# Three edits to a two-block fp32 kernel on one core: semaphores cleared inside the next stage, the meta products of attention moved, the last expert units loaded into free places

## The chip, the cores and the metric

The kernel runs on 1 core of one Trainium2 chip. The metric is the device time of one execution in microseconds.

## The reference

Two transformer blocks in a row, fp32, batch 1, 512 tokens, width 1024. The first has stick-breaking attention (8 heads of 64) beside a gated linear attention (4 heads of 128), 16 meta tokens ahead of the sequence, and a mixture of 32 experts with two experts for each token. The second has a convolution branch, a state-space branch and a dense feed-forward part. Cut to what the change touches:

```python
def stick_breaking_attention(q, k, v):
    ...
        z = einsum('bhtd,bhsd->bhts', q[:, :, t0:t1], k[:, :, :t1]) * scale
        valid = (s_pos < t_pos) & (s_pos >= LEAD_PAD)
        log_keep = where(valid, log_sigmoid(-z), 0.0)
        log_tail = cumsum(log_keep, axis=3, reverse=True) - log_keep
        w = where(valid, exp(log_sigmoid(z) + log_tail), 0.0)
        outs.append(einsum('bhts,bhsd->bhtd', w, v[:, :, :t1]))

def hierarchical_moe(x2, ...):
    ...
    def run_block(args):
        tok, g, e = args
        xb = x2[tok]
        hb = silu(xb @ w_gate[e]) * (xb @ w_up[e])
        return (hb @ w_down[e]) * g[:, None]
```

## The kernel before

The program is a row of ten stages. Each is one `nc.Block()` in which SyncE (SP), ScalarE (ACT), VectorE (DVE), GpSimd (POOL) and TensorE (PE) have a program of their own and wait for one another by semaphores. They are: projections of the first block (block at L148), stick-breaking attention (L467), gated linear attention (L738), output projection and routing (L1000), the 32 experts (L1336), overflow blocks of the experts (L1563), the join of the two blocks (`join`, L1853), the groups of the state-space branch (L1990), the mix (L2550) and the feed-forward part (`ffn`, L2806). A block ends with a drain on each engine and a barrier in which GpSimd collects and releases the others. The profile puts these under the line where the stage's sources begin: L101 for the first stage, L1299 for the experts, L1554 for the overflow.

Behind each stage stands `g["clear"](...)` (L2904 to L2914): another block, in which GpSimd alone clears every semaphore of the stage, one instruction each (L2911), while the others go straight into that block's barrier (L2907). Then the semaphores go back to the pool, and the next stage takes them. The semaphores on which the gathers and scatters count (`g["gathers"]`) are cleared but not given back.

Attention (L418 to L712) works through 24 pieces, three per head. For a piece, TensorE forms the scores (`scores`, L479 a mask product, L484 products over 64 rows), ScalarE turns them into log terms (`front`, L553 to L557), VectorE adds (`sums`, L649 and L655), TensorE forms the sums over later keys by triangular matrices (`tails`, L492 to L507), ScalarE takes the exponential (`weights`, L572), and TensorE multiplies by the values (`values`, L519). Three pieces are kept in flight (AHEAD = 3), with six banks. The scores of the 16 meta keys of all heads are formed at once (L527, four fp32 products of 512 columns), and their values are spread (L530); both stand on TensorE between the first three `scores` and the loop, and their parts on ScalarE (`front_meta`, L561 to L565) and VectorE (`sums_meta`, `values_meta`, L659 and L664) stand at the same place. TensorE waits for five constants of GpSimd (`con`) ahead of the loop. ScalarE takes the logs of the forget gates (`log_forget`, L575) in the pieces 0 to 3; VectorE reads them from piece 6 on (`decays`).

The expert stage (L1294 to L1547) takes an expert's weights in six units of 1 MB: 0 and 1 of the gate, 2 and 3 of the up, 4 and 5 of the down matrix. Each unit number has its own place for the raw fp32 (`raw_e`), for the high part and for the low part. SP loads a unit when VectorE has made the low part of that place's last unit (L948). ScalarE copies it to the high part (`hi`, L1354), which waits until TensorE has used the place's last unit; VectorE subtracts (`lo`, L1422). TensorE runs, for expert e: `project` of the gate (L1498, L1499), `combine` of expert e-1 (L1512), the turning of the gathered rows (L1489), `project` of the up matrix, `down` of expert e-2 (L48 to L50). `down` waits for `y_out` of the expert before (L1394, ScalarE), and GpSimd gathers rows (L1460) and scatters the result (L1464). The loops run on after the last expert until nothing is left, so on ScalarE the end reads:

```python
for e in range(E + 3):
    hi(e + 1, 0); gate_out(e); hi(e - 2, 5); silu(e - 1); hi(e + 1, 1); y_out(e - 3)
    gathered(e + 1); hi(e + 1, 2); h_hi(e - 1); hi(e + 1, 3); up_out(e); hi(e - 1, 4)
```

The overflow stage reads on each engine, from `over_e`, how many overflow blocks there are, and passes over its body if there are none.

Of the kernel before, what the change touches and what calls it, by code (L numbers as in the profile page):

```python
# [5 lines left out]
ALU = mybir.AluOpType  # L6
# [10 lines left out]
NT = T // P  # L17
# [53 lines left out]
def stage_a(nc, dram, g, sem, banks):  # L71
# [5 lines left out]
    with ExitStack() as keep:  # L77
# [361 lines left out]
        with ExitStack() as tmp:  # L439
# [30 lines left out]
            def _(pe):  # L470
# [59 lines left out]
                mm(O, pick[:, :, :].rearrange("k h s -> k (h s)"), v_nat[0:META, NT, :], start=True, stop=True).then_inc(s["vr"], 1)  # L530
                pe.wait_ge(s["con"], 5)
                for n in range(NP):
                    if n + AHEAD < NP:
                        scores(n + AHEAD)
                    tails(n)
                    if n % 3 == 0 and n >= 3:
                        values(n // 3 - 1)
# [8 lines left out]
            def _(act):  # L546
# [34 lines left out]
                front_meta()  # L581
                for n in range(NP):
# [3 lines left out]
                    if n < HG_HEADS:  # L586
                        log_forget(n)
# [11 lines left out]
            def _(pool):  # L599
                gp = nc.gpsimd  # L600
# [32 lines left out]
            def _(dve):  # L633
# [84 lines left out]
        with ExitStack() as tmp:  # L718
# [138 lines left out]
            def _(pool):  # L857
                nc.gpsimd.memset(acc, 0.0).then_inc(s["cleared"], 1)
# [63 lines left out]
def stage_b(nc, dram, g, sem, banks):  # L922
# [23 lines left out]
    def load(sp, j, of):  # L946
        place = raw_e[j][:, :] if j < 4 else raw_e[j][:, :].rearrange("p (k c) -> p k c", k=2)
        sp.dma_start(place, unit_source(of, j)).then_inc(s_raw_e[j], 16)  # L948
# [7 lines left out]
    with ExitStack() as tmp:  # L956
# [66 lines left out]
        def _(pool):  # L1023
            nc.gpsimd.iota(iota[:, :], [[1, P]], 0, 0, allow_small_or_imprecise_dtypes=True).then_inc(s["io"], 1)
# [274 lines left out]
    with ExitStack() as tmp:  # L1299
# [24 lines left out]
        def made_hi(e, j):  # L1324
            return (s["ghi"], 4 * e + j + 1) if j < 4 else (s["dhi"], 2 * e + j - 3)

        def made_lo(e, j):
            return (s["glo"], 4 * e + j + 1) if j < 4 else (s["dlo"], 2 * e + j - 3)
# [7 lines left out]
        block = tmp.enter_context(nc.Block())  # L1336

        @block.sync
        def _(sp):
            for e in range(E + 2):  # L1340
                for at, j in ((e + 1, 0), (e - 2, 5), (e + 1, 1), (e + 1, 2), (e + 1, 3), (e - 1, 4)):
                    if 1 <= at < E:
                        sp.wait_ge(*made_lo(at - 1, j))
                        load(sp, j, at)

        @block.scalar
        def _(act):
            def hi(e, j):

                if 0 <= e < E:  # L1350
# [1608 lines left out]
```

## Time and profile before

| what | value |
|---|---|
| times of three runs, us | 2415.74, 2419.7, 4282.94 |
| median, us | 2419.7 |
| the profiled execution's own time, us | 2418.91 |
| its span, us | 2417.2 |
| mean granted clock of TensorE | 0.92 |
| busy: TensorE / its weight loads / VectorE / ScalarE / GpSimd | 87% / 69% / 58% / 45% / 8% |
| DMA, mean over the span | 144 GB/s |

The profile records one execution. Its span is counted from the first to the last instruction; the execution's own time is 1.7 us longer. Times in rows are us from the start of the span unless they are marked ns. Drains, semaphore instructions and DMA issues are not counted as busy. PE is TensorE's matmul, PEld its weight load; a letter q behind an engine's name is its instruction queue. A granted clock of 1.00 is 2.4 GHz, 0.50 is 1.2 GHz. A row for a stretch of time has its length, then for PE, PEld, DVE, ACT and POOL the busy time and in brackets the count of instructions, then the granted clock, the share in which the DMA engines were busy, and GB/s. A row in order of time begins with start and duration, and may end with the idle time before it and what ended that. A row for the instructions of one line has count, shortest/median/longest in ns, and the starts of the first and the last.

### The profile page before, as it was taken

Reading aid. Unit: us, or ns where it says so; the run is one execution under the profiler, and the core shown is the slowest. Engines: PE = TensorE matmul, PEld = TensorE weight load, DVE = VectorE, ACT = ScalarE, POOL = GpSimd, SP = SyncE. Lnnn points to the kernel's source line nnn. Section 1 sums busy time; section 2 is a strip of 40 time slices with the busy share of each in tenths; the row PEclk is TensorE's granted clock in tenths of the full one; section 3 lists DMA queues with packets and bytes.
Section 4 is the critical chain, followed back from the end, with each engine's and each line's share of the span. In section 5 each row is a group of like instructions: output and inputs, shape, how many; then the busy total and the mean of one; then the engine's idle time right before and its main releaser. Section 6 shows DMA issues by size and latency. Waiting matters only on the chain. (4 is left out here: it accounts for less than half of the span.)

```text
span 2417.2 us, 25574 instructions
## 1 busy us (share of the span) xinstructions
PE 2097.0 (87%) x10228; PEld 1665.3 (69%) x10228; DVE 1391.7 (58%) x1512; ACT 1084.2 (45%) x1229; POOL 189.0 (8%) x132
## 2 busy tenths in 40 slices
PE   5999966675899999993779999997698987999997
PEld 4886546563666666662668888886567866888786
DVE  4111468346899989883339898887733244333223
ACT  4232632224788888882333555544243224222212
POOL 0001021000222212220000000000000000000000
PEclk9998987766999999996689999998899998999999
DMA  4220000414999999984233333323132222333231
GB/s 153 70 70 1 1 0 1 160 61 183 380 399 406 405 401 402 401 337 167 53 89 87 91 102 88 87 71 87 35 105 87 87 70 74 92 105 87 87 105 52
DMA packets 202064, 346.89 MB, mean 144 GB/s; under 512 B 13872, under 2 KB 149544, under 8 KB 184536
## 3 DMA queue, kind: packets, MB, share of 16 engines
q1 hardware_dynamic: 191280, 332.49, 39.3%
q0 software_dynamic: 5120, 8.40, 1.1%
q10 hardware_dynamic: 5543, 4.34, 0.6%
q8 instruction: 82, 1.34, 0.2%
q14 instruction: 39, 0.31, 0.0%
HBM read 340.93 MB, written 12.65 MB: 146 GB/s over the span
## 5 line engine op out<-in xcount | busy, mean ns | idle before, releaser
L1422 DVE TENSOR_TENSOR wlo_e<-raw_e,whi_e 128x2048 fp32r<-128x2048 f32 x192 | 436.3, 2289 | 62.5 <-ACT whi_e L1354 62.2
L1354 ACT CAST whi_e<-raw_e 128x2048 fp32r<-128x2048 f32 x192 | 366.8, 1913 | 77.3 <-PE pall L1499 37.6
L1717 DVE TENSOR_TENSOR w_lo<-w_raw,w_hi 128x2048 fp32r<-128x2048 f32 x89 | 203.8, 2290 | 322.0 <-ACT w_hi L1709 322.0
L48 PE MATMUL pall<-hT_hi,w_lo 128*128 128x512 f32 x864 | 348.2, 403 | 26.8 <-DVE xbc L2255 10.3
L1709 ACT CAST w_hi<-w_raw 128x2048 fp32r<-128x2048 f32 x89 | 169.4, 1904 | 429.4 <-PE pall L50 414.9
L49 PE MATMUL pall<-hT_lo,w_hi 128*128 128x512 f32 x864 | 342.4, 396 | 0.0
L50 PE MATMUL pall<-hT_hi,w_hi 128*128 128x512 f32 x864 | 341.8, 396 | 0.0
L1498 PE MATMUL pall<-whi_e,xs 128*128 128x512 f32 x512 | 208.6, 407 | 9.3 <-DVE wlo_e L1422 4.9
L48 PEld LDWEIGHTS pall<-hT_hi,w_lo 128*128 128x128 f32 x864 | 166.3, 193 | 63.8 <-DVE xbc L2255 10.6
L1499 PE MATMUL pall<-wlo_e,xs 128*64 128x512 f32 x512 | 204.4, 399 | 0.0
L49 PEld LDWEIGHTS pall<-hT_lo,w_hi 128*128 128x128 f32 x864 | 166.3, 192 | 34.9 <-issue 0.5
L50 PEld LDWEIGHTS pall<-hT_hi,w_hi 128*128 128x128 f32 x864 | 165.9, 192 | 35.4
L1498 PEld LDWEIGHTS pall<-whi_e,xs 128*128 128x128 f32 x512 | 98.5, 192 | 60.3 <-issue 8.5
L2240 DVE SCALAR_TENSOR_TENSOR mixed<-yT,cols,mixed 128x512 f32<-128x512 f32 x180 | 126.4, 748 | 0.0
L48 PE MATMUL pall<-whi_e,hT_lo 128*64 128x512 f32 x256 | 101.6, 397 | 7.2 <-ACT mixed L1394 4.5
L48 PE MATMUL pall<-w_hi,hT_lo 128*128 128x256 f32 (+1 forms) x320 | 98.9, 309 | 9.6 <-DVE hT_lo L2697 9.0
L50 PE MATMUL pall<-whi_e,hT_hi 128*64 128x512 f32 x256 | 102.0, 399 | 0.0
L49 PE MATMUL pall<-wlo_e,hT_hi 128*64 128x512 f32 x256 | 101.7, 397 | 0.0
L1460 POOL DMA_INDIRECT xg<-m_rows,row_x x32 | 84.0, 2625 | 184.9 <-DVE xg L1416 137.8
L50 PE MATMUL pall<-w_hi,hT_hi 128*128 128x256 f32 (+1 forms) x320 | 97.8, 306 | 0.0
L49 PE MATMUL pall<-w_lo,hT_hi 128*128 128x256 f32 (+1 forms) x320 | 97.8, 306 | 0.0
L2850 DVE TENSOR_TENSOR mixed<-mixed,pall 128x512 f32<-128x512 f32 x22 | 15.1, 688 | 142.6 <-PE pall L50 142.6
(483 smaller groups left out, 3922.8 us busy)
## 6 DMA issues: line engine op xcount, KB each, us to landing
raw_e<-in_w_expert_up_dram SPq DMA_DIRECT2D x64, 1024.0 KB, 11.1
raw_e<-in_w_expert_down_dram SPq DMA_DIRECT2D x64, 1024.0 KB, 11.6
raw_e<-in_w_expert_gate_dram SPq DMA_DIRECT2D x64, 1024.0 KB, 11.3
w_raw<-in_w_in_dram SPq DMA_DIRECT2D x80, 512.0 KB, 5.8
w_raw<-in_w_gate_up_dram SPq DMA_DIRECT2D x44, 512.0 KB, 5.1
w_raw<-in_w_down_dram SPq DMA_DIRECT2D x22, 512.0 KB, 4.1
mixed<-in_w_in_dram SPq DMA_DIRECT2D x10, 1024.0 KB, 5.0
A<-acs_rows SPq DMA_DIRECT2D x8, 1024.0 KB, 4.9
```

The lines of the kernel that those rows point to most:

```text
L48: nc.tensor.matmul(out, w_lo, m_hi, start=start, stop=False)
L49: nc.tensor.matmul(out, w_hi, m_lo, start=False, stop=False)
L50: return nc.tensor.matmul(out, w_hi, m_hi, start=False, stop=stop)
L1354: nc.scalar.copy(whi[j][:, :], raw[j][:, :]).then_inc(made_hi(e, j)[0], 1)
L1422: nc.vector.tensor_tensor(wlo[j][:, :], raw[j][:, :], whi[j][:, :].bitcast(F32), ALU.subtract).then_inc(made_lo(e, j)[0], 1)
L1460: pool.indirect_dma_start(xg[0:SLOTS, :], None, m_rows, bass.IndirectOffsetOnAxis(row_x[0:SLOTS, b:b + 1], 0), bounds_check=T - 1, oob_is_ ...
L1498: mm(out, x[:, kk, :], k4(whi[j])[:, k, :], start=kk == 0, stop=False, skip_group_check=True)
L1499: last = mm(out[0:SLOTS, :], x[:, kk, 0:SLOTS], k4(wlo[j])[:, k, :], start=False, stop=kk == KD - 1, skip_group_check=True)
L1709: self.nc.scalar.copy(self.hi[i][:, :], self.raw[i][:, :]).then_inc(self.s_hi, 1)
L1717: (engine or self.nc.vector).tensor_tensor(self.lo[i][:, :], self.raw[i][:, :], self.hi[i][:, :].bitcast(F32), ALU.subtract).then_inc(self ...
L2240: ins = V.scalar_tensor_tensor(mixT[:, c, :], src, col("dw_w_a", k * KD + c), mixT[:, c, :], ALU.mult, ALU.add)
L2850: V.tensor_tensor(hd, sg, banks[(2 * c + 1) % 8], ALU.mult).then_inc(s["hd"], 1)
```

## The change

1. `clear` no longer makes a block. It notes the stage's semaphores in `stale`, and the new `sweep`, which stands first in GpSimd's program of each following stage, clears them there, one instruction per run of neighbouring numbers. They are given back one stage later. Stages without a GpSimd program get one that only sweeps. One last block at the end clears what is left.
2. In attention, the meta products (TensorE) stand behind `tails(0)`; `front_meta`, `sums_meta` and `values_meta` stand at the matching place of piece 0, and `log_forget` moves from the pieces 0 to 3 to the pieces 2 to 5.
3. Units 5 of expert 30 and 4 and 5 of expert 31 use the places of units 0, 1 and 2 (`LATE`), as if these belonged to an expert 32. SP, ScalarE and VectorE get an end written out after a loop of 32 turns.
4. The blocks of the expert and the overflow stage end without a drain on GpSimd.

```diff
@@ attention: TensorE, ScalarE, VectorE
                 for n in range(AHEAD):
                     scores(n)
-                pe.wait_ge(s["kb"], 1)
-                for c in range(4):
-                    last = mm(ZM, kb[:, c, :], qT[:, c, :], start=c == 0, stop=c == 3, skip_group_check=True)
-                last.then_inc(s["zm"], 1)
-                pe.wait_ge(s["vb"], 1)
-                mm(O, pick...).then_inc(s["vr"], 1)
                 pe.wait_ge(s["con"], 5)
                 for n in range(NP):
                     if n + AHEAD < NP:
                         scores(n + AHEAD)
                     tails(n)
+                    if n == 0:
+                        pe.wait_ge(s["kb"], 1)
+                        for c in range(4):
+                            last = mm(ZM, kb[:, c, :], qT[:, c, :], start=c == 0, stop=c == 3, skip_group_check=True)
+                        last.then_inc(s["zm"], 1)
+                        pe.wait_ge(s["vb"], 1)
+                        mm(O, pick...).then_inc(s["vr"], 1)
                     if n % 3 == 0 and n >= 3:
                         values(n // 3 - 1)
...
                 for n in range(AHEAD):
                     front(n)
-                front_meta()
                 for n in range(NP):
                     if n + AHEAD < NP:
                         front(n + AHEAD)
                     weights(n)
-                    if n < HG_HEADS:
-                        log_forget(n)
+                    if n == 0:
+                        front_meta()
+                    if 2 <= n < 2 + HG_HEADS:
+                        log_forget(n - 2)
...
-                sums_meta()
-                values_meta()
                 for n in range(NP):
                     if n + AHEAD < NP:
                         sums(n + AHEAD)
+                    if n == 0:
+                        sums_meta()
+                        values_meta()
@@ every later stage
             @block.gpsimd
             def _(pool):
+                g["sweep"](pool)
@@ experts
+        LATE = {(E - 2, 5): (E, 0), (E - 1, 4): (E, 1), (E - 1, 5): (E, 2)}
         def used(e, j):
+            e, j = LATE.get((e, j), (e, j))
             return (s["gused"], 4 * e + j + 1) if j < 4 else (s["dused"], 2 * e + j - 3)
...
-        block = tmp.enter_context(nc.Block())
+        block = tmp.enter_context(nc.Block(no_gpsimd_drain=True))
         @block.sync
         def _(sp):
-            for e in range(E + 2):
+            for e in range(E):
                 for at, j in ((e + 1, 0), (e - 2, 5), (e + 1, 1), (e + 1, 2), (e + 1, 3), (e - 1, 4)):
                     if 1 <= at < E:
                         sp.wait_ge(*made_lo(at - 1, j))
                         load(sp, j, at)
+            for (at, j), (turn, place) in LATE.items():
+                sp.wait_ge(*made_lo(turn - 1, place))
+                load(sp, j, at, place)
...
-            for e in range(E + 3):
+            for e in range(E):
                 hi(e + 1, 0)
...
+            hi(E - 2, 5)
+            silu(E - 1)
+            y_out(E - 3)
+            hi(E - 1, 4)
+            h_hi(E - 1)
+            hi(E - 1, 5)
+            y_out(E - 2)
+            y_out(E - 1)
...
+            lo(E - 2, 5)
+            hidden(E - 1)
+            lo(E - 1, 4)
+            h_lo(E - 1)
+            lo(E - 1, 5)
...
+                            at = LATE.get((e, j), (e, j))[1]
                             last = split_mm(nc, Y[half][0:SLOTS, :], hT_hi[e % 2][:, kk, :], hT_lo[e % 2][:, kk, :],
-                                            k2(whi[j])[:, k, c], k2(wlo[j])[:, k, c], kk == 0, kk == 3)
-                    last.then_inc(s["dused"], 1)
+                                            k2(whi[at])[:, k, c], k2(wlo[at])[:, k, c], kk == 0, kk == 3)
+                    last.then_inc(used(e, j)[0], 1)
@@ build
+        stale, swept = [], []
         def clear(named, *lists):
-            done = list(named.values()) + [x for group in lists for x in group]
-            with nc.Block() as block:
-                @block.gpsimd
-                def _(pool):
-                    for x in done:
-                        pool.sem_clear(x)
-            for x in done:
+            for x in swept:
                 if x not in g["gathers"]:
                     nc.release_semaphore(x)
+            swept.clear()
+            stale.extend(x for x in list(named.values()) + [x for group in lists for x in group] if x not in g["gathers"])
+
+        def sweep(pool):
+            nums = sorted(x.num for x in stale)
+            first = 0
+            for n in range(1, len(nums) + 1):
+                if n == len(nums) or nums[n] != nums[n - 1] + 1:
+                    pool.sem_clear(range(nums[first], nums[n - 1] + 1))
+                    first = n
+            swept.extend(stale)
+            stale.clear()
```

## Rows read from the trace of the kernel before

**Rows 1.** The page, its first part: busy time of each engine.
```profile
PE 2097.0 (87%) x10228; PEld 1665.3 (69%) x10228; DVE 1391.7 (58%) x1512; ACT 1084.2 (45%) x1229; POOL 189.0 (8%) x132
```

**Rows 2.** Instructions of L2911: in all, at boundaries 1 and 8, the last.
```profile
L2911 POOLq EVENT_SEMAPHORE_RANGE_CLEAR  x291: 37/38/47, 224.2 to 2416.8; - x146
...
L2911 POOLq EVENT_SEMAPHORE_RANGE_CLEAR  x38: 37/38/47, 224.2 to 226.5; - x38
...
L2911 POOLq EVENT_SEMAPHORE_RANGE_CLEAR  x55: 37/38/38, 1751.5 to 1755.0; - x55
...
L2911 POOLq EVENT_SEMAPHORE_RANGE_CLEAR  x19: 37/38/38, 2415.7 to 2416.8; - x19
```

**Rows 3.** Instructions of L101 and L2907 at the first boundary.
```profile
L101 SPq EVENT_SEMAPHORE  x1: 17/17/17, 224.1 to 224.1; - x1
...
L2907 POOLq DRAIN  x1: 41/41/41, 226.6 to 226.6; - x1
...
L2907 SPq EVENT_SEMAPHORE  x1: 17/17/17, 226.8 to 226.8; - x1
```

**Rows 4.** Stretches of time around the start of attention and within it.
```profile
223.40:226.90 3.50, 0.00 (x0) 0.00 (x0) 0.00 (x0) 0.53 (x2) 0.00 (x0) 0.87 0.00 0
...
226.90:239.60 12.70, 12.67 (x18) 5.51 (x19) 5.06 (x15) 6.21 (x10) 10.49 (x19) 0.50 0.01 2
...
239.60:252.00 12.40, 12.40 (x40) 6.17 (x40) 4.37 (x8) 10.83 (x20) 0.00 (x0) 1.00 0.00 0
...
260.00:290.00 30.00, 30.00 (x132) 18.43 (x132) 16.99 (x37) 17.22 (x35) 0.00 (x0) 1.00 0.00 1
```

**Rows 5.** In order of time: TensorE and VectorE in attention.
```profile
226.93 0.66 PE L479 MATMUL pall<-keep_r,ident_r 128*128 128x384 f32 x1 [3.64 <-PEq L2907]
...
229.10 0.69 PE L479 MATMUL pall<-keep_r,ident_r 128*128 128x384 f32 x1
...
231.43 0.29 DVE L655 TENSOR_TENSOR qq<-qq 128x128 f32<-128x128 f32 x1
...
241.48 0.45 PE L479 MATMUL pall<-keep_r,ident_r 128*128 128x384 f32 x1
...
242.70 0.59 PE L492 MATMUL pall<-qq,from_on 128*128 128x384 f32 x1
```

**Rows 6.** A stretch of the experts' middle; loads and ScalarE at their end.
```profile
700.00:800.00 100.00, 99.24 (x505) 68.38 (x504) 93.09 (x58) 87.54 (x76) 28.41 (x13) 1.00 1.02 405
...
1081.61 15.95 SPq L948 DMA_DIRECT2D raw_e<-in_w_expert_down_dram  x4
...
1103.49 1.90 ACT L1354 CAST whi_e<-raw_e 128x2048 fp32r<-128x2048 f32 x1 [0.86 <-PE pall L50]
...
1105.29 1.00 ACT L1394 COPY mixed<-pall 64x1024 f32<-64x1024 f32 x1
```

**Rows 7.** Stretches of time at the end of the expert stage.
```profile
1094.50:1096.10 1.60, 0.07 (x1) 0.02 (x1) 1.23 (x1) 1.51 (x3) 0.00 (x0) 1.00 0.49 54
...
1103.40:1106.40 3.00, 0.01 (x1) 0.04 (x1) 2.54 (x2) 2.81 (x2) 0.00 (x0) 1.00 0.00 0
...
1106.60:1110.00 3.40, 3.40 (x9) 1.79 (x8) 1.11 (x1) 0.00 (x0) 1.42 (x1) 0.50 0.16 35
```

**Rows 8.** Instructions of L1299, the expert stage's end.
```profile
L1299 POOLq DRAIN  x1: 5286/5286/5286, 1118.3 to 1118.3; - x1
...
L1299 SPq EVENT_SEMAPHORE  x1: 17/17/17, 1123.7 to 1123.7; - x1
```

**Rows 9.** In order of time: one gather; and the page's group of all.
```profile
629.97 7.24 POOL L1460 DMA_INDIRECT xg<-m_rows,row_x  x1 [0.31 <-issue]
...
631.91 9.11 DVE L1422 TENSOR_TENSOR wlo_e<-raw_e,whi_e 128x2048 fp32r<-128x2048 f32 x4
...
643.96 1.41 PE L1489 MATMUL pall<-ident,xg 128*128 128x128 f32 x8 [5.98 <-DMA xg<-m_rows,row_x]
...
L1460 POOL DMA_INDIRECT xg<-m_rows,row_x x32 | 84.0, 2625 | 184.9 <-DVE xg L1416 137.8
```

More of the change, by code:

```diff
@@ L535, in _ @@
                     tails(n)
+                    if n == 0:
[4 more added lines that the diff above has]
+                        pe.wait_ge(s["vb"], 1)
+                        mm(O, pick[:, :, :].rearrange("k h s -> k (h s)"), v_nat[0:META, NT, :], start=True,
+                           stop=True).then_inc(s["vr"], 1)
                     if n % 3 == 0 and n >= 3:
@@ L944, in unit_source, with load @@
         return w_down[:, bass.ds(e, 1), k:k + 2, :].rearrange("p o k f -> p (o k) f")
-    def load(sp, j, of):
-        place = raw_e[j][:, :] if j < 4 else raw_e[j][:, :].rearrange("p (k c) -> p k c", k=2)
-        sp.dma_start(place, unit_source(of, j)).then_inc(s_raw_e[j], 16)
+    def load(sp, j, of, slot=None):
+        slot = j if slot is None else slot
+        place = raw_e[slot][:, :] if j < 4 else raw_e[slot][:, :].rearrange("p (k c) -> p k c", k=2)
+        sp.dma_start(place, unit_source(of, j)).then_inc(s_raw_e[slot], 16)
     s = {n: sem("d_" + n) for n in (
@@ L1318, in stage_b @@
         turned = XT.rearrange("p (k t) -> p k t", k=KD)
+        LATE = {(E - 2, 5): (E, 0), (E - 1, 4): (E, 1), (E - 1, 5): (E, 2)}
         def used(e, j):
+            e, j = LATE.get((e, j), (e, j))
             return (s["gused"], 4 * e + j + 1) if j < 4 else (s["dused"], 2 * e + j - 3)
         def made_hi(e, j):
+            e, j = LATE.get((e, j), (e, j))
             return (s["ghi"], 4 * e + j + 1) if j < 4 else (s["dhi"], 2 * e + j - 3)
         def made_lo(e, j):
+            e, j = LATE.get((e, j), (e, j))
             return (s["glo"], 4 * e + j + 1) if j < 4 else (s["dlo"], 2 * e + j - 3)
@@ L1350, in hi @@
                 if 0 <= e < E:
+                    sem_hi = made_hi(e, j)[0]
+                    e, j = LATE.get((e, j), (e, j))
                     act.wait_ge(s_raw[j], 16 * e + 16)
@@ L1353, in hi @@
                         act.wait_ge(*used(e - 1, j))
-                    nc.scalar.copy(whi[j][:, :], raw[j][:, :]).then_inc(made_hi(e, j)[0], 1)
+                    nc.scalar.copy(whi[j][:, :], raw[j][:, :]).then_inc(sem_hi, 1)
             def gathered(e):
@@ L1421, in lo @@
                     dve.wait_ge(*made_hi(e, j))
+                    sem_lo = made_lo(e, j)[0]
+                    e, j = LATE.get((e, j), (e, j))
                     nc.vector.tensor_tensor(wlo[j][:, :], raw[j][:, :], whi[j][:, :].bitcast(F32),
-                                            ALU.subtract).then_inc(made_lo(e, j)[0], 1)
+                                            ALU.subtract).then_inc(sem_lo, 1)
             def gathered(e):
@@ L1445, in _ @@
                 lo(0, j)
-            for e in range(E + 2):
+            for e in range(E):
                 lo(e + 1, 0)
@@ L1562, in stage_b @@
         y = sb("y_o", [P, D])
-        block = tmp.enter_context(nc.Block())
+        block = tmp.enter_context(nc.Block(no_gpsimd_drain=True))
         def blocks(eng, turn):
@@ L1828, in stage_c @@
         join(nc, dram, g, sem, banks, W, hT)
+        g["stale"].extend(g["gathers"])
         with ExitStack() as ssm:
@@ L1861, in _ @@
                 W.load(sp, u)
+        @block.gpsimd
+        def _(pool):
+            g["sweep"](pool)
         @block.scalar
@@ L2037, in _ @@
         def _(pool):
+            g["sweep"](pool)
             for i in range(NV):
@@ L2576, in _ @@
                 W.load(sp, u)
+        @block.gpsimd
+        def _(pool):
+            g["sweep"](pool)
         @block.scalar
@@ L2816, in _ @@
                 sp.wait_ge(x, 16 * NT // 2)
+        @block.gpsimd
+        def _(pool):
+            g["sweep"](pool)
         @block.scalar
@@ L2893, in ffn, with _ @@
     g["clear"](s, W.sems(), s_out)
+    with nc.Block() as block:
+        @block.gpsimd
+        def _(pool):
+            g["sweep"](pool)
 def build(nc, dram, out):
@@ L2920, in build @@
              "mixed": sb("mixed", [P, NT, D]), "eps": sb("eps", [P, 2]), "pall": pall}
-        g["clear"] = clear
+        g["clear"], g["sweep"], g["stale"] = clear, sweep, stale
         g["gathers"] = []
```

5 lines of the change are left out of this document (4 added, 1 removed).

## The prediction, made before the change was run

> **What bounds the kernel now.** I read the page first. TensorE is busy for 87% of a span of 2417.2 us [rows 1], so a stage is worth what its last wait is worth, and I looked for places where TensorE, or every engine, stands still. The program is ten stages in a row, and each ends in a barrier. So I went to the instructions of the clearing block next, which the page does not count as busy. Between two stages GpSimd issues one clear per semaphore while the other four engines wait: 291 clears in the program, 38 after the first stage, 55 after the eighth, 19 at the very end [rows 2]. The first boundary shows the parts. Its stage releases the engines at 224.1, GpSimd's own drain comes at 226.6 behind the last clear, and the engines are released again at 226.8 [rows 3]. That is 2.7 us in which nobody computes.
>
> Then the stage that follows the first boundary, by stretches and in order of time: TensorE does nothing from 223.4 to 226.9, then is busy for 12.67 of 12.70 us at a granted clock of 0.50 (1.2 GHz), then busy throughout at 1.00 (2.4 GHz), also much later in the stage [rows 4]. So this stage hangs on TensorE alone.
>
> Last the end of the expert stage. In its middle the DMA engines are busy without a break at 405 GB/s [rows 6], and the change does not touch that. At its end it is a chain over TensorE and ScalarE, and after the last scatter has landed GpSimd spends 5286 ns, from 1118.3 on, in a drain before the barrier opens at 1123.7 [rows 8].
>
> **The change part by part.**
>
> *Clears.* Nine boundaries go. The 55 clears run from 1751.5 to 1755.0, so 3.5/54 = 0.065 us each; 272 of the 291 stand ahead of the last block: 272 x 0.065 = 17.7 us. To it come 0.3 us per boundary for the drain and second barrier (last clear 226.5, release 226.8): 2.7 us. Together 20.4 us [rows 2, 3]. What takes their place is a few range clears at the head of GpSimd's next program. For each run of numbers I take the price of one clear, 0.065 us. In the attention stage they stand ahead of the memset that VectorE's first copy needs, but that copy ends long before the first use, which waits for ScalarE; in the overflow stage GpSimd's program ends ahead of TensorE's. Cost 0; without that cover 0.1 to 0.3 us per boundary, 1 to 3 us in all. Does anything land or get loaded under the clears, so that it is late now? A stage issues its first loads after the boundary, so these move up with it, and the units that are prefetched over a boundary were issued tens of us earlier. I take the whole 20.4 us; bounds 17 and 21. In the last block 19 clears become a few: (19 - 2) x 0.065 = 1.1 us.
>
> *Clock at the start of attention.* TensorE idles there for 3.6 us now, and the clock falls. Without the clears 1.0 us remains at most (TensorE's last product ends just ahead of 223.4, the release is at 224.1, and the first product of a stage stands 0.1 behind its release) [rows 3 to 5]. In this trace a fall came after idle stretches of 1.6 us and of 3.0 us [rows 7]; none as short as 1.0 us between busy stretches led to one that I found. So I take it that the clock stays at 1.00. The price: a first piece takes 229.10 - 226.93 = 2.17 us at 0.50 and the same piece 242.70 - 241.48 = 1.22 us at 1.00 [rows 5], a factor of 1.78. 12.7 us become 7.1: 5.6 us. Other engines don't take the bound over: ScalarE is busy 17.2 and VectorE 17.0 us of 30 where TensorE has no gap [rows 4]. Bounds: 5.6 gained, or 1.7 lost if the clock falls and, with the heavy meta products later in the order, rises later by as much as the half-speed stretch of 3.4 us at the end of the expert stage lasts (half of it is lost) [rows 7].
>
> The Trainium skill ("TensorE: Matmul & The Clock Gate", section "What's actually happening") speaks against this term: throttled is the default, and activity releases it. The first pieces of attention are products over 64 of 128 rows, and at 0.50 they did not bring the clock up in 7 us although TensorE was busy [rows 4, 5]. If light work also lets it fall, the term is 0 or below; that is the first rival, and its time is worked out below from rows. By the page the sum below would be 30.5 us or less.
>
> *Meta scores behind the first triangular product.* The meta products change places with the fourth scores and the first tails. Nothing goes. TensorE has no gap before or after; the operand of the first tails is ready at 231.7 [rows 5], before TensorE gets there; ScalarE waits for the meta products now, but that is not on the path. The logs of the forget gates move two pieces down, and their reader comes at the seventh piece. I take 0; bounds -1 and +2.
>
> *Last down units in free places.* The loads of three units now wait for places that are free by 1080 and are issued at about 1082 behind the one of 1081.6, where before the four issues of the end were spread from 1081.6 to 1097.6 [rows 6]. ScalarE's queue: the cast of the last unit stood at 1103.49 behind the use of its old place, and the copy of the output sums of expert 30, whose product had ended at 1103.4, began behind it at 1105.29 and ended at 1106.29 [rows 6]. For it expert 31's product waited from 1103.4 to 1106.4 [rows 7]. With its own place the cast runs at about 1098, the copy begins at 1103.3, and the product at 1104.4: 2.0 us. VectorE's halves are then ready by 1103. What is late next is that copy of 1.0 us itself. The idle stretch shrinks from 3.0 to 1.0 us, so I take the second half-speed stretch as gone too: 3.4 / 2 = 1.7 us [rows 7]. Sum 3.7; bounds 0 and 5.4 (if the first slow stretch goes as well). Three more loads of 1 MB in flight meet a DMA queue that is no longer full there.
>
> *No drain.* 5.3 us on the path [rows 8]. Nothing in the trace shows GpSimd going on to other instructions without a drain. Bounds: 5.3 gained, or 0 if the engine holds its next instruction as long. I take 5.3, because the scatters' semaphores had been counted before the drain began. The next drain, where anything outstanding would be paid, is that of the join stage, in which GpSimd has nothing to do and ends first.
>
> The Trainium skill ("PSUM — Partial Sum Buffer", section "Engine vs sequencer instructions") says that a sequencer instruction waits only until earlier ones are dispatched, while a drain waits for the engine to be idle. By that the 5.3 us would be gone for good; no row here shows it.
>
> **Sum.** 20.4 + 1.1 + 5.6 + 0 + 3.7 + 5.3 = 36.1 us. The profiled execution took 2418.9 us (span 2417.2), 0.8 us less than the median of the three, 2419.7; one of these is 4283 us, far outside and not explained by anything I read. 2418.9 - 36.1 = 2382.8, say 2383 us, 1.5% less.
>
> **The rivals.**
> - *The clock falls at the start of attention all the same.* For it: the light first pieces, above. Against it: later in the stage the same pieces among heavier products keep 1.00. 2383 + 5.6 = 2388.6, with the late rise 2390.
> - *The drain is paid elsewhere*, by GpSimd's clears or its register load in the overflow stage, for whose end all wait. 2383 + 5.3 = 2388.
> - *The late units don't do what they should*: a load or a cast still waits for the old place, or the copy still stands behind a cast. 2383 + 3.7 = 2387.
> - *The clears were cover.* If half of it returns as waits for first loads or code at the new stages: 2383 + 10 = 2393. For it: each stage starts with dependent first steps. Against it: in the first boundary TensorE's first product comes 0.1 us behind the release.
> - *Slower than before.* In the expert loop one gather took 7.24 us to be issued where the mean of 32 is 2.6 [rows 9], while VectorE ran four of its low-part subtractions back to back for 9.11 us, and TensorE then waited 5.98 us for it [rows 9]. The shift of the phases could bring this more often. At 6.0 us each it decides from the seventh on (6 x 6.0 = 36): 7 give 2383 + 42 = 2425. Against it: the loop starts from the same state as before, one case in 32 gathers. The other way, if the one case goes, the time is 2377.
>
> **How the numbers follow.** The forecast 0.58 (with 0.10 of it at 2377 or less), the clock 0.18, the drain 0.10, the late units 0.05, the cover 0.06, slower than before 0.03. The range: down to 2368, where the stretched gather goes (-6), the first slow stretch too (-1.7) and a few half-speed stretches end sooner; up to 2400, where clock and drain fail together (2395) and a few half-speed stretches elsewhere end 3.4 us later. A difference of 2%, 48 us, is about what a measurement of this kernel can tell from none. 2% less is 2371: faster 0.07, from the forecast's low end; slower by as much needs 14 stretched gathers: 0.01; within 2% 0.92.
>
> **What would show it.** Right: no clearing block but the last; about 0.1 us from a stage's release to the next stage's first product; granted clock 1.00 from the end of the first stage through the first 12 us of attention; the fourth scores and first tails ahead of the meta products; TensorE's gap between the last two down products 1.0 us at full clock behind it; the expert stage's barrier 0.3 us behind the landing of the last scatter. Wrong: a half-speed stretch at the start of attention; GpSimd's first clear or load of the overflow stage lasting 5 us; first products of the stages that wait for a load or for a code fetch; more than one gather of over 5 us.

## The result, and the profile after

| | before | after |
|---|---|---|
| median, us | 2417.7 (four runs, one of them 4283) | 2384.7 (four runs, 2383.3 to 2388.7) |
| ratio, 95% interval | | 0.9875 (0.9849 to 0.9902): within 2% |
| profiled execution: its time / span, us | 2418.9 / 2417.2 | 2388.7 / 2386.9 |

The forecast was 2383. The run of 4283 us is a slow one that stands apart; without it the median before is 2415.7 us and the difference 31.0. Two later sets of runs of the same kernel on other chips gave 2384.9 (ratio 0.9872) and 2386.3 (0.9870), 31.1 and 31.4 us below the kernel before on the same chips. So the gain is some 31 us or 1.3%. The time is near the forecast, but the gain is 5 us short of the 36.1 that was forecast: one step failed in nearly every profile.

The page of the changed kernel, first part, answers to [rows 1]: the same work in a shorter span.

```profile
PE 2097.7 (88%) x10228; PEld 1667.3 (70%) x10228; DVE 1391.0 (58%) x1512; ACT 1084.0 (45%) x1229; POOL 190.1 (8%) x132
```

The instructions of the sweep's line, the only clears left (count, then shortest, median and longest in ns). They answer to [rows 2]: 20 in place of 291, and nothing waits for them.

```profile
L2973 POOLq EVENT_SEMAPHORE_RANGE_CLEAR  x20: 43/77/329, 224.8 to 2386.5; - x20
its engine sat idle before it (us, times) until:
who waited for it (us, times):
```

The attention stage begins so, TensorE in order of time, against [rows 3, 5]:

```profile
224.84 0.41 PE L479 MATMUL pall<-keep_r,ident_r 128*128 128x384 f32 x1 [0.94 <-PEq L101]
...
229.97 0.69 PE L479 MATMUL pall<-keep_r,ident_r 128*128 128x384 f32 x1
230.59 1.65 PE L484 MATMUL pall<-qT,kT 64*128 64x256 f32 x4
232.16 1.65 PE L492 MATMUL pall<-qq,from_on 128*128 128x384 f32 x2
233.60 0.64 PE L494 MATMUL pall<-qq,before 128*128 128x128 f32 x2
234.03 5.33 PE L533 MATMUL pall<-qT,kb 128*128 128x512 f32 x8
```

The idle is 0.94 us where it was 3.64, and the first product stands 0.1 us behind the release (224.7). The fourth scores and the first tails are ahead of the meta products. But look at the lengths: the piece at 229.97 takes 0.69 us, as its like did at half clock before. The stretches of time say it plainly (length, then busy time of PE, PEld, DVE, ACT, POOL, granted clock, DMA share, GB/s), against [rows 4]:

```profile
224.70:227.30 2.60, 2.46 (x9) 1.39 (x9) 1.57 (x8) 2.38 (x4) 2.10 (x9) 0.99 0.00 0
227.30:237.50 10.20, 10.20 (x18) 4.84 (x18) 4.34 (x10) 5.74 (x11) 8.39 (x10) 0.50 0.01 2
237.50:252.00 14.50, 14.50 (x55) 7.72 (x53) 4.37 (x8) 9.46 (x17) 0.00 (x0) 1.00 0.00 0
```

TensorE starts at full clock, and 2.4 us after its first product, busy all the time, falls to half for 10.2 us. Before, it was 13.7 us. So the stage from release to release is only 1.1 us shorter (105.6 to 104.4).

The end of the expert stage: ScalarE and GpSimd in order of time, then TensorE between the last two down products, against [rows 6, 7]:

```profile
1090.38 1.92 ACT L1371 CAST whi_e<-raw_e 128x2048 fp32r<-128x2048 f32 x1
1094.22 1.01 ACT L1411 COPY mixed<-pall 64x1024 f32<-64x1024 f32 x1 [1.91 <-PE pall L50]
1101.06 1.01 ACT L1411 COPY mixed<-pall 64x1024 f32<-64x1024 f32 x1 [5.84 <-PE pall L50]
...
1102.84 0.90 POOL L1497 DMA_INDIRECT y_rows<-mixed,row_y  x1 [5.95 <-ACT mixed L1411]
...
1093.78 0.40 PE L50 MATMUL pall<-whi_e,hT_hi 128*64 128x512 f32 x1
1095.32 0.41 PE L48 MATMUL pall<-whi_e,hT_lo 128*64 128x512 f32 x1 [1.14 <-issue]
```

The last cast ends at 1092.3, the copy no longer stands behind it, and TensorE's gap is 1.14 us where it was 3.0. The products behind it take 0.40 us each, which is full clock. Then the stage's end and the next drain, lines L1307 and L1880, against [rows 8]:

```profile
L1307 SPq EVENT_SEMAPHORE  x2: 17/17/17, 1074.8 to 1105.8; - x2
...
L1880 POOLq DRAIN  x1: 5302/5302/5302, 1107.8 to 1107.8; - x1
```

The release is the second of SyncE's two. The last scatter's landing is counted at 1105.4 and the release is at 1105.8. The drain is not gone: it runs at the head of the join stage, 5302 ns where it was 5286, beside a stage that ends at 1149.9. Nobody waits for it there.

By stages, from release to release, the 30.2 us between the two profiled spans are: nine boundaries 20.65; last block 0.65; attention 1.1; experts 7.15 (561.7 to 554.6); all others together 0.6 (the groups 1.8 shorter, the mix 1.7 longer, the rest below 0.8 each).

### The profile page after: what moved, and what is told of

The parts are those of the page before. It is cut to its first block and busy times, and to the rows that moved or that the text cites. A ratio compares the mean times of both kernels' runs of the same rounds, so it can differ in the third digit from the quotient of the medians.

```text
span 2386.9 us, 25210 instructions
## 1 busy us (share of the span) xinstructions
PE 2097.7 (88%) x10228; PEld 1667.3 (70%) x10228; DVE 1391.0 (58%) x1512; ACT 1084.0 (45%) x1229; POOL 190.1 (8%) x132
## 6 DMA issues: line engine op xcount, KB each, us to landing
raw_e<-in_w_expert_down_dram SPq DMA_DIRECT2D x64, 1024.0 KB, 11.6
```

## The experiments

All ratios are to the kernel before, with 95% intervals; medians that are compared directly come from runs on one chip.

**The sweep alone.** The kernel before with the clears and their barriers taken away and the range clears put in, meta order, late units and GpSimd's drain as before.

```
         def _(pool):
+            g["sweep"](pool)
...
```

> The kernel before with the clears moved into the next stage alone. Theory (the boundaries and the last block are worth what the two traces show between a stage's release and the next, 20.6 us, and 0.7 at the end; the clock of attention falls now and then all the same): about 21 us less than before, 19 to 27. Rival (the clears covered something that comes back as waits): 10 us less or under. By the term of the prediction for the clock, were it right: 26 us less.

Measured: 2391.8 us, ratio 0.9895 (0.9874 to 0.9917), 24.4 below before by medians. The profile has attention at 102.8 us, with 6.8 us at half clock; 20.65 for the boundaries, 2.8 for attention and 1.0 for the last block make up the gain. So the clears carry the largest part of the gain, and something of the clock comes with them.

**The late units alone.** The kernel before with the last three down units loaded into free places.

```
+        LATE = {(E - 2, 5): (E, 0), (E - 1, 4): (E, 1), (E - 1, 5): (E, 2)}
...
+            for (at, j), (turn, place) in LATE.items():
+                sp.wait_ge(*made_lo(turn - 1, place))
+                load(sp, j, at, place)
```

> The kernel before with the late units in free places alone, with the drain. Theory: the stretch from the last combine to the end of the last output copy shrinks from 22.0 to about 17 us, 2 us of it from the copy that no longer stands behind a cast, the rest from half-speed stretches that do not come; the whole 3 to 5 us less. Rival (what the changed kernel shows at its end comes from the missing drain or from chance in the clock): 0 to 2 us less.

Measured: 2414.1 us, ratio 0.9987 (0.9968 to 1.0007), 2.2 us below the median of the kernel before on that chip (2416.2). By the times this is not told from nothing, so I read the stage. Without its drain it is 548.7 us (554.0 - 5.3), where two kernels without the late units, as free of a long gather as this one (that matters, below), have 553.1 and 553.6: 4.4 to 4.9 us. What was expected of the stage's end came: from the last weight load of the last `combine` to the end of the last output copy it is 15.3 us where the kernel before has 20.5. TensorE's gap there is that of the changed kernel, and both half-speed stretches of 3.4 us that the kernel before has at its end (from 1096.4 and from 1106.6) are missing:

```profile
1101.20 0.42 PE L48 MATMUL pall<-whi_e,hT_lo 128*64 128x512 f32 x1 [1.14 <-issue]
```

The start of attention, whose code this kernel has as before, shows a half-speed stretch of 10.2 us and takes 104.4 us, exactly as in the first profile of the changed kernel; behind 3.64 us of idle the clock was still 1.00 at the first product and fell 0.6 us later. So the kernel before, too, has the shorter stretch in one of its three profiles:

```profile
228.30:229.00 0.70, 0.58 (x2) 0.43 (x3) 0.00 (x0) 0.62 (x1) 0.25 (x1) 1.00 0.00 0
229.00:239.30 10.30, 10.30 (x15) 4.13 (x15) 5.05 (x15) 5.59 (x10) 9.97 (x19) 0.50 0.01 2
```

**The meta order alone**, in the kernel before, and **undone**, in the changed kernel.

```
                     tails(n)
+                    if n == 0:
+                        pe.wait_ge(s["kb"], 1)
...
```

> The kernel before with the meta products behind the first tails alone. Theory (TensorE has no gap on either side, so a change of order gives nothing): attention 105.6 us as before, between 1.7 less and 1.7 more by where the clock rises; the whole within 2 us. Rival (ScalarE, which waited 4.5 us for the meta products, gains its lead and the stage gets shorter): attention 2 to 5 us shorter.

> The changed kernel with its second part undone: the meta scores and value rows ahead of the ordinary ones again. What the move is worth. My estimate was 0 (bounds 1 us worse to 2 us better for the move), so the time should lie within 2 us of the changed kernel's. The rival, that the move is what brought the first products down to the release: then TensorE would wait at the start of attention for the meta keys' copy, and the time would be 3 to 5 us above the changed kernel.

Measured: alone 2418.2 us, 2.0 above the median before on that chip, ratio 1.0004 (0.9991 to 1.0018), attention 105.7 us against 105.6. Undone 2385.1 us against 2384.9 for the changed kernel on the same chip, attention 102.9 against 102.8. The move is worth nothing that these runs can show. The rival, that it brought the first products down to the release, is out: undone, the first product still comes 0.94 us behind the last one, 0.1 behind the release. ScalarE's gain of 2 to 5 us did not come either.

**The drain put back.** The changed kernel with GpSimd's drain at the end of the expert and overflow stages; run twice, the second time on one chip with the changed kernel.

```
-        block = tmp.enter_context(nc.Block(no_gpsimd_drain=True))
+        block = tmp.enter_context(nc.Block())
...
```

> The changed kernel with GpSimd's drain back at the end of the expert and the overflow stage. Theory (a fixed price on the path): the drain takes 5.3 us, and the whole is 5.3 us above the changed kernel, 27 to 28 us below the one before. Rival (the drain only waits for what GpSimd has to finish anyway, and would be shorter or paid elsewhere): no more than 2 us above the changed kernel.

> GpSimd's drains put back, once more: the first run of this gave a median 10 us above the changed kernel, on another chip. If a drain that nothing covers costs its own 5.3 us and nothing else, the time is 5 to 6 us above the changed kernel on this chip; if it also moves what follows (a transfer, a longer stretch at half clock in the join), 8 to 11 us.

Measured: 2394.7 us, ratio 0.9906 (0.9873 to 0.9940), and the second time 2390.9 us against 2386.3 for the changed kernel: 4.6 us. The first median is 21.6 us below the kernel before on its chip, where 27 to 28 were expected, and the chip had no runs of the changed kernel to set it against. It is also 2.9 us above the sweep alone on that chip, although it has the late units besides; its profile has a gather of 7.2 us that the sweep's has not (below). Why it came some 5 us high is not shown. The second median needs nothing beyond the drain. The second run's profile, line L1307:

```profile
L1307 POOLq DRAIN  x1: 5292/5292/5292, 1107.6 to 1107.6; - x1
L1307 SPq EVENT_SEMAPHORE  x1: 17/17/17, 1113.0 to 1113.0; - x1
```

The same profile shows something else, at the start of attention (as above, by stretches):

```profile
224.70:227.30 2.60, 1.66 (x7) 1.04 (x6) 0.65 (x3) 2.05 (x3) 1.23 (x5) 1.00 0.00 0
227.30:240.00 12.70, 12.70 (x35) 5.60 (x34) 7.11 (x18) 10.12 (x20) 9.26 (x15) 1.00 0.01 1
```

The same instructions in the same order as in the changed kernel, behind the same idle of 0.94 us, and the clock never falls. The stage takes 99.6 us.

**Filler products.** The changed kernel with six dense products at the start of attention; then the same with 64 rows in place of 128.

```
+                fill(2)
                 for n in range(AHEAD):
                     scores(n)
+                    if n < 2:
+                        fill(2)
```

> The changed kernel once more, on the chip that the next two share. Both theories: about 30 us below the kernel before (ratio 0.9875, some 2387 us where the kernel before takes 2417). Theory A (the 0.9 us idle and the scores of 64 rows together make the clock fall at the start of attention): the stretch at half clock there begins at some place between 226 and 229 us, as in the first profile (227.3), and is 7 to 13 us long; how long it is moves from execution to execution by some us. Theory B (the idle alone): the same.

> The changed kernel with six dense 128x512 products (128 rows, on a bank that holds nothing yet) set in at the start of attention: two ahead of the first scores, two behind the first and two behind the second; six by some 0.21 us at full clock = 1.3 us of added work. Theory A (the scores of 64 rows that follow the idle make the clock fall): the granted clock stays 1.00 through the first 12 us of attention, the half-speed stretch of 10.2 us is gone, which gives back half of it, 5.1 us; net 3.8 us below the changed kernel. Theory B (the idle alone makes it fall, whatever follows): the clock falls at the same place, and the time is 1.3 to 2.6 us above.

> The filler products of e7_fill with 64 rows in place of 128: the same count, the same duration, the engine just as busy. Theory A (the 64 rows of the scores make the clock fall): the half-speed stretch is back at the start of attention, 6.8 us or more, and the time is 3 to 5 us above that of e7_fill, so at or a little above the changed kernel. Theory B (what saved the clock in e7_fill was that the idle ended a little sooner, or that the heavy products of the meta row came at another moment): no stretch at half speed, the time of e7_fill, 2381 us.

Measured: 2381.4 us (ratio 0.9866, 0.9850 to 0.9883) against 2384.9 (0.9872) for the changed kernel on that chip; with 64 rows 2387.3 against 2386.3 on another chip. The changed kernel on the first of these chips, without filler, has the shorter half-speed stretch, later than in the first profile:

```profile
228.70:235.50 6.80, 6.80 (x13) 3.39 (x12) 3.71 (x8) 5.04 (x10) 6.67 (x8) 0.50 0.01 2
```

With the 128-row filler, by stretches:

```profile
224.70:227.30 2.60, 2.44 (x10) 1.64 (x10) 1.55 (x7) 1.93 (x3) 2.10 (x9) 1.00 0.00 0
227.30:240.00 12.70, 12.70 (x36) 5.90 (x36) 5.79 (x13) 9.66 (x19) 8.39 (x10) 1.00 0.01 1
```

The half-speed stretch is gone, and attention takes 101.0 us against 102.8: 1.8 of the 3.5 us between the medians. But it is gone with the 64-row filler too:

```profile
223.00:227.00 4.00, 3.06 (x12) 1.90 (x11) 0.69 (x3) 1.88 (x2) 1.26 (x5) 1.00 0.00 0
227.00:240.00 13.00, 13.00 (x40) 6.18 (x38) 6.46 (x17) 9.50 (x18) 9.21 (x14) 1.00 0.01 1
```

Here attention takes 101.2 us, but the median is no better than the changed kernel's. So theory A, as it was put, missed: the rows of the filler did not decide. Theory B of the first filler, that the idle alone makes the clock fall whatever follows, is contradicted by both filler profiles and by the drain's second run. Theory B of the second was right on the clock and missed on the time, 2387.3 for 2381; of its two reasons one is out, since the idle is 0.94 us with each filler too. What stays: of the eight profiles with the 0.94 us idle and no filler seven show the fall; of the three with filler (the third is below) none does. The single profile of the 64-row filler can be luck, as the drain's run shows, so what decides whether the clock falls is left open.

**Filler in the join too.** The changed kernel with the 128-row filler, and transposes behind each tile's eight in the join stage.

```
+                for k in range((8, 3, 4, 3)[i]):
+                    nc.tensor.transpose(banks[5][:, 0:P], xn[i][:, 0:P], ident[:, :])
```

> The changed kernel again, to share a chip with the next three: 2382 to 2388 us, with a half-clock stretch of 6.8 to 10.2 us in the first 15 us of attention.

> e7_fill, and in the join stage behind each tile's eight transposes 8, 3, 4 and 3 transposes more of what is at hand, into a bank that nobody reads, in gaps where TensorE waits. They are to bring the clock up before the groups' stage begins: of the 51.2 us at half clock the last 5.3 lie in the groups' stage and give back 2.6 us, and the later transposes and their casts come some 1.5 us sooner. Expected: 4 us below e7_fill, 8 below the changed kernel, some 2377 us. Rival: the extra transposes delay the real ones by up to 1 us a tile and the clock rises only behind the release: 1 to 3 us above e7_fill.

Measured: 2384.8 us against 2386.3 for the changed kernel on that chip, ratio 0.9855 (0.9828 to 0.9882), with runs at 2377, 2378, 2381 and at 2389, 2390, 2393. The join did not do what it should:

```profile
1133.40:1150.70 17.30, 11.63 (x50) 10.12 (x50) 14.90 (x19) 10.82 (x16) 0.00 (x0) 0.50 0.00 1
1150.70:1155.40 4.70, 4.63 (x11) 3.70 (x12) 0.00 (x0) 0.00 (x0) 0.30 (x4) 0.50 0.83 181
```

TensorE is busy for 11.6 of 17.3 us with the filler, the clock stays at 0.50, and it rises only 4.7 us into the next stage (4.5 in the changed kernel of this set). The join takes 42.8 us in both. Expectation missed, filler without effect here. The gap between the two triples of runs is told below.

**A drain in the middle of the expert loop.**

```
                 if e + 1 < E:
                     pool.wait_ge(s["xt"], e + 1)
+                    if e == 16:
+                        nc.gpsimd.drain()
                     gather(e + 1)
```

> The changed kernel with one more drain of GpSimd inside the experts' loop, ahead of the seventeenth expert's successor's gather. Theory C (a drain behind indirect transfers has a fixed price): it lasts 5.3 us there too, and the one in the join stage lasts 5.3 us again. Theory D (it works off something for each indirect transfer since the last drain): the middle one lasts about 2.7 us and the one in the join about 2.6 us. The loop is bound by the weights' stream, so the span moves by less than 3 us in either case, unless the late gather delays the token products.

The two drains in that profile, lines L1506 and L1882:

```profile
L1506 POOLq DRAIN  x1: 8208/8208/8208, 811.8 to 811.8; - x1
...
L1882 POOLq DRAIN  x1: 2840/2840/2840, 1105.4 to 1105.4; - x1
```

The join's drain fell from 5302 to 2840 ns: theory C, a fixed price, is out. From the middle drain on, the profile has 34 indirect transfers, in the whole stage 64: 2840/34 and 5302/64 are both 83 ns per transfer. The middle one is longer than its share (8.2 against some 2.5 us) and was not taken apart; a scatter was being issued when it began. So the 83 ns rest on two drains, and a third does not fit by itself. The span was 2384.7 us. The expert stage takes 551.5 us where the changed kernel has 548.9 in a profile as free of a long gather, so of the 8.2 us most fell into slack.

**Long gathers.** No experiment was made for this; it is read from the profiles of the others. In some the longest gather of the loop took 2.9 or 3.0 us, in others 4.9, 7.2 or 11.6, always a single one. Here is a gather of ordinary length, from the changed kernel of the second set, with VectorE beside it in order of time. The gather begins ahead of VectorE's copy `xs`, which reads PSUM:

```profile
617.44 2.23 POOL L1493 DMA_INDIRECT xg<-m_rows,row_x  x1 [0.31 <-issue]
...
618.77 0.68 DVE L1455 TENSOR_TENSOR xs<-pall,xs 128x512 fp32r<-128x512 f32 x1
...
621.91 8.89 DVE L1449 TENSOR_TENSOR wlo_e<-raw_e,whi_e 128x2048 fp32r<-128x2048 f32 x4
```

The same gather in the profile of the 64-row filler begins behind that copy:

```profile
617.25 11.65 POOL L1501 DMA_INDIRECT xg<-m_rows,row_x  x1 [0.30 <-issue]
...
616.05 0.68 DVE L1463 TENSOR_TENSOR xs<-pall,xs 128x512 fp32r<-128x512 f32 x1
616.65 2.28 DVE L1457 TENSOR_TENSOR wlo_e<-raw_e,whi_e 128x2048 fp32r<-128x2048 f32 x1
618.85 0.42 DVE L1475 TENSOR_TENSOR hT_lo<-hidT,hT_hi 128x256 fp32r<-128x256 f32 x1
619.18 8.89 DVE L1457 TENSOR_TENSOR wlo_e<-raw_e,whi_e 128x2048 fp32r<-128x2048 f32 x4
627.99 0.41 DVE L1470 TENSOR_TENSOR hidT<-sgT,pall 128x256 f32<-128x256 f32 x1
...
635.02 1.41 PE L1530 MATMUL pall<-ident,xg 128*128 128x128 f32 x8 [10.31 <-DMA xg<-m_rows,row_x]
```

From 616.65 to 627.99 VectorE runs nothing but subtractions with both operands in SBUF, without a gap. The gather ends at 628.90, 0.9 us behind the start of the first instruction that reads PSUM again, and TensorE waits 10.31 us for its tokens. From 628.1 its granted clock is then 0.50 for 13.7 us, which is part of the price:

```profile
628.10:641.80 13.70, 6.78 (x21) 4.64 (x22) 3.20 (x3) 2.89 (x3) 3.50 (x3) 0.50 0.94 359
```

In the profile shown at the top the block has a gap in its middle:

```profile
619.05 7.24 POOL L1493 DMA_INDIRECT xg<-m_rows,row_x  x1 [0.30 <-issue]
...
620.98 4.49 DVE L1449 TENSOR_TENSOR wlo_e<-raw_e,whi_e 128x2048 fp32r<-128x2048 f32 x2
626.11 4.57 DVE L1449 TENSOR_TENSOR wlo_e<-raw_e,whi_e 128x2048 fp32r<-128x2048 f32 x2 [0.65 <-ACT whi_e L1371]
```

VectorE pauses at 625.47, and the gather ends at 626.29. This looks as if a gather had to wait until VectorE pauses or reads PSUM, but the profiles do not bear that out. In the profile of the middle drain the same gather begins at the same place, 0.5 us behind the end of `xs`, with the same subtractions beside it:

```profile
619.37 2.50 POOL L1493 DMA_INDIRECT xg<-m_rows,row_x  x1 [0.30 <-issue]
...
618.16 0.68 DVE L1455 TENSOR_TENSOR xs<-pall,xs 128x512 fp32r<-128x512 f32 x1
618.77 2.28 DVE L1449 TENSOR_TENSOR wlo_e<-raw_e,whi_e 128x2048 fp32r<-128x2048 f32 x1
620.97 0.42 DVE L1467 TENSOR_TENSOR hT_lo<-hidT,hT_hi 128x256 fp32r<-128x256 f32 x1
621.30 4.49 DVE L1449 TENSOR_TENSOR wlo_e<-raw_e,whi_e 128x2048 fp32r<-128x2048 f32 x2
```

It ends at 621.87, 0.8 us behind the end of the first subtraction, with the next ones already running; VectorE pauses only at 625.79. Most gathers are of this kind: in the fourteen profiles 348 of 448 begin in a low-part subtraction and end 0.8 us behind its end, though `hT_lo` follows it without a pause. The long ones end 0.8 us behind the end of a subtraction too, but of a later instruction: the second (4.9 us), the fourth (7.2) or the sixth (11.6). In the run with the meta order undone there is no pause at that point either. These are nine of the 448, each the fifth or sixth of its loop. What lets a gather through at the first end or only at a later one is open.

The Trainium skill ("SBUF — State Buffer", section "SBUF: two separate sides") describes such a trap: while VectorE holds the port pair that it shares with GpSimd, GpSimd can't write the descriptors of its transfers. The traces agree in kind, in that the end of a gather hangs on the end of a VectorE instruction; the Trainium skill has about 0.1 us from the release to the end where they have 0.8. No run isolates the cause. What it costs, by the expert stage (the drain taken off where it lies in the stage, so all with the late units):

| longest gather, us | expert stage, us | profiles |
|---|---|---|
| 2.9 to 3.0 | 548.7, 548.9 | late units alone; changed kernel, second set |
| 4.9 | 551.2 | filler, 128 rows |
| 7.2 | 550.8, 551.3, 551.4, 554.6 | changed kernel, first set; meta undone; drain back; the first profile after |
| 11.6 | 557.7, 558.3, 558.6 | filler, 64 rows; drain back, second; join filler |

The middle drain's profile (2.9, 551.5) is left out of the table, since its loop is another. From the first row to the last it is some 9 us. The length is not all: the first profile after lies 3 us above the others of its row, and nothing here says why. The 9 us are as wide as the gap between the two triples of the join filler, whose profiled run had the 11.6; that the slower triple had it too was not seen, since only one run of each kernel is profiled.

Is the long gather this change's doing? Of the three profiles without the sweep one has it (before, 7.2), of the eleven with the sweep eight. That is too few to say, and no run separates it.

## Why the prediction was right or wrong

**Clears: right.** Forecast 20.4, and the nine boundaries, from release to release in the profile before, add up to 20.65; in each new stage TensorE's first product comes as soon behind the release as before or sooner (0.1 us in five of the nine), so nothing came back in their place, and the rival that they were cover is out. The last block gave 0.65 instead of 1.1 us. The price of one clear, 0.065 us, was too low for a range, whose median is 0.077 and longest 0.33, but that is 0.1 us here: the two ranges take 0.24 us where the 19 clears took 1.22. The rest is that GpSimd's first clear there comes 0.4 us behind its last release signal, and 0.1 before.

**Clock: the failed step.** The prediction said "none as short as 1.0 us between busy stretches led to one that I found. So I take it that the clock stays at 1.00". The idle was 0.94 us as forecast, and the clock fell in seven of eight profiles without filler. It falls 2.4 to 3.1 us after the first product, while TensorE is busy; the step looked for a fall in the idle and not behind it. The price per us of half clock was right:

| half clock at the start, us | attention, us |
|---|---|
| 13.7 (before; meta order alone) | 105.6, 105.7 |
| 10.2 (after; late units alone) | 104.4, 104.4 |
| 6.8 (six profiles) | 102.8 to 102.9 |
| none (drain back, second) | 99.6 |

From the first row to the last 6.0 us, where 5.6 was forecast for the whole; from 13.7 to 6.8 us at half clock it is 2.8, and that is what the change usually brings (two of the three profiles without it have the 13.7, six of eight with it the 6.8). The first rival, at 0.18, is closer to what happened than the forecast: its condition came true, its price half. The prediction cited the Trainium skill against its own term and yet weighed it at one in six. The Trainium skill ("TensorE: Matmul & The Clock Gate", section "What's actually happening") also says that the number of slow products differs from run to run of one kernel; the table agrees: each of its last three rows holds a profile of the changed attention, with the same instructions.

**Meta order: right**, 0 forecast. By attention's length the move costs 0.1 us in the kernel before, and undoing it costs 0.1 us in the changed one: inside what one execution differs from the next.

**Late units: the mechanism right, the size low.** The gap and the clock came as told (1.14 us, full clock). The prediction took one of the two half-speed stretches as gone and left the other to the bound; both went, in the profile after as in that of the late units alone. Forecast 3.7, upper bound 5.4, measured 4.4 to 4.9 by the stage's length in profiles. The times show less, 2.2 us, with an interval that holds 0.

**Drain: right**, 5.3 us off the path (4.6 by medians on one chip) and paid where nobody waits. The argument through the join stage held. What did not hold in it is the thought of a debt of what is outstanding: the scatters had long landed when the join's drain took its 5302 ns. The Trainium skill ("PSUM — Partial Sum Buffer", section "Engine vs sequencer instructions") gave the direction: overflow's first instructions, a range clear of 67 ns and a register load of 0.50 us as before, did not wait.

**The slower rival** had an event that exists and the wrong number of cases: it wanted seven long gathers and there was never more than one, but that one costs from 2 to 9 us, where I had 6. Its reason, subtractions of VectorE back to back, is not enough: in most gathers they stand there too. Whether the change brings that one more often stays open. It is a large part of why the changed kernel's profiles scatter by more than the smaller terms.

The sum with what was measured: 20.65 + 0.65 + 2.8 - 0.1 + 4.6 + 5.3 = 33.9 us, against 31.0 to 31.4 between medians. The forecast's 36.1 was too high by the clock term (2.8) and too low by the late units (0.9); the two together are 2 us. Another 2.5 to 3 us are not settled by these runs. The late units may be part of it: with medians alone, sweep 24.4, late units 2.2 and drain 4.6 make 31.2. The long gather, none in some profiles and 11.6 in others, is wide enough for it, and so is gated linear attention, which no part of the change was to move and which takes 86.3 to 90.9 us from profile to profile.

That the forecast of 2383 lies only 1.7 us from 2384.7 is in part luck: it was taken off a profiled execution of 2418.9 us, 3 us above the median of the runs before, and that hid more than half of the 5 us that the gain fell short.

## What to carry to other kernels

Clear semaphores inside the next stage's program, on an engine with slack, and let an indirect-transfer engine's drain fall where its next stage is idle: these two gave 26 of the 31 us and came out as the rows said. When a forecast rests on the granted clock, read the clock behind a short idle, not only in it, and count the outcome as a spread over executions. When one profile of a stage disagrees with the next by some us, look for a single long instruction on GpSimd and at what VectorE ran beside it.

## What the hardware showed that was not expected

- GpSimd's drain behind indirect transfers lasted 83 ns for each transfer since the last drain in two drains (64: 5.30 us, 34: 2.84 us), in the first although the last had landed 2.4 us earlier. One that began beside a scatter lasted longer (8.2 us behind 30).
- The clock can fall 2.4 to 3.1 us after TensorE has resumed behind 0.94 us of idle, and the same instructions keep it in another execution. With six products of 512 columns set in there it stayed in three profiles of three.
- An indirect gather beside VectorE's subtractions with both operands in SBUF ended 0.8 us behind the end of one of them, 2.5 to 2.9 us after its start in most cases, but 4.9, 7.2 or 11.6 us in nine of 448, where it passed over one, three or five ends.
- TensorE busy for 11.6 of 17.3 us with transposes of 128 columns kept 1.2 GHz throughout.
